# GpSimd in place of VectorE for scaling the softmax probabilities and for the differential subtraction, in a two-block transformer kernel on one core

## The reference, cut to what matters

```python
# differential heads (4 heads, two maps each, per layer)
p = jax.nn.softmax(s, axis=-1)
a = p[:, 0] - lam * p[:, 1]
return jnp.einsum('bhqs,bshd->bqhd', a.astype(v.dtype), v)
...
# latent (mla), cross (x) and grouped (gqa) heads; windowed (swa) heads add exp(sink - m) to the sum
p = jax.nn.softmax(s, axis=-1)
return jnp.einsum('bhqs,bshd->bhqd', p.astype(v.dtype), v)
```

## Time and profile before

| what | value |
|---|---|
| median of 3 runs | 1756.21 us (1754.52 to 1757.25) |
| span of the profiled execution | 1752.8 us |
| what lies around that span | not given for this execution; the median less its span is 3.4 us |
| PE busy | 1572.7 us (90%) |
| DVE busy | 802.2 us (46%) |
| ACT busy | 374.8 us (21%) |
| POOL busy | 2.2 us |
| HBM read | 383.65 MB |

### The profile page before, as it was taken

The page is one execution under the profiler, slowest core; times in us unless marked ns, Lnnn a source line. Parts: engine busy times, 40 slices in busy tenths (PEclk is TensorE's granted clock), DMA queues, the critical chain, the costliest instruction groups (busy, mean ns, idle before and its releaser), DMA issues.

```text
span 1752.8 us, 25923 instructions
## 1 busy us (share of the span) xinstructions
PE 1572.7 (90%) x10722; PEld 1084.5 (62%) x10722; DVE 802.2 (46%) x1623; ACT 374.8 (21%) x943; POOL 2.2 (0%) x6
## 2 busy tenths in 40 slices
PE   9999999999999999999999999999999656656666
PEld 5877878884488786888648778888853112112111
DVE  6686567665577765766646575242421000000001
ACT  4362131110325422311002561111211000000001
POOL 0000000000000000000000000000000000000000
PEclk9999999999999999999999999999999977788767
DMA  9324335444542241544444223221888999999997
GB/s 394 127 73 168 121 121 209 160 177 173 201 169 94 96 169 72 203 174 162 177 172 162 103 100 119 74 73 53 335 337 329 427 423 424 425 425 426 423 421 326
DMA packets 49472, 386.35 MB, mean 220 GB/s; under 512 B 5584, under 2 KB 6096, under 8 KB 9808
## 3 DMA queue, kind: packets, MB, share of 16 engines
q1 hardware_dynamic: 47376, 375.15, 54.0%
q10 hardware_dynamic: 1984, 9.57, 1.4%
HBM read 383.65 MB, written 1.05 MB: 219 GB/s over the span
## 4 chain that ended last, share of the span: by engine, by line
PE 72%; DMA 21%; DVE 3%; ACT 2%; issue 1%; DVEq 0%; SPq 0%; ACTq 0%
PE ps L212 52%; DMA arena<-in_stream 21%; PE ps L2347 3%; PE ps L1090 2%; PE ps L1579 2%; PE ps L216 1%; PE ps L1189 1%; PE ps L739 1%; PE ps L1222 1%; PE ps L1248 1%; PE ps L1680 0%; PE ps L640 0%; PE ps L2429 0%; PE ps L1030 0%; PE ps L2486 0%
## 5 line engine op out<-in xcount | busy, mean ns | idle before, releaser
L212 PE MATMUL ps<-arena 128*128 128x256 f32 (+4 forms) x2364 | 532.7, 491 | 88.0 <-DMA arena<-in_stream 78.3
L212 PEld LDWEIGHTS ps<-arena 128*128 128x128 f32 (+1 forms) x2364 | 308.5, 172 | 270.9 <-DMA arena<-in_stream 131.5
L212 PE MATMUL ps<-ring,arena 128*128 128x256 f32 (+5 forms) x1172 | 319.1, 497 | 35.3 <-DMA ring<-in_stream 29.4
L212 PE MATMUL ps<-arena,ring 128*128 128x256 f32 (+1 forms) x1212 | 274.4, 374 | 0.0
L212 PEld LDWEIGHTS ps<-ring,arena 128*128 128x128 f32 (+1 forms) x1172 | 177.7, 173 | 150.9 <-issue 75.4
L212 PEld LDWEIGHTS ps<-arena,ring 128*128 128x128 f32 x1212 | 216.2, 191 | 35.5 <-issue 9.6
L2906 DVE TENSOR_TENSOR arena<-arena,ps 128x512 f32<-128x512 f32 x8 | 5.5, 687 | 308.9 <-PE ps L2684 308.9
L2684 PE MATMUL ps<-arena 128*32 128x512 f32 x218 | 139.8, 769 | 0.0
L1137 ACT ACTIVATE arena<-arena,small 128x256 f32<-128x256 f32 x112 | 55.7, 498 | 67.0 <-DVE small L1124 50.5
L1726 ACT ACTIVATE arena<-arena 128x512 f32<-128x512 f32 x20 | 12.6, 630 | 179.4 <-DVE arena L1782 179.4
L1090 PE MATMUL ps<-arena 64*128 64x256 f32 (+3 forms) x256 | 46.8, 392 | 0.8 <-DVE arena L1120 0.5
(11 more groups left out here) (461 smaller groups left out, 1994.5 us busy)
## 6 DMA issues: line engine op xcount, KB each, us to landing
ring<-in_stream SPq DMA_DIRECT2D x131, 1024.0 KB, 4.9
arena<-in_stream SPq DMA_DIRECT2D x112, 1024.0 KB, 13.0
arena<-in_stream SPq DMA_DIRECT2D x24, 2048.0 KB, 37.2
ring<-in_stream SPq DMA_DIRECT2D x12, 2048.0 KB, 32.4
spare<-in_stream SPq DMA_DIRECT2D x6, 2048.0 KB, 37.0
par<-in_stream SPq DMA_DIRECT2D x8, 1024.0 KB, 38.7
const<-in_stream SPq DMA_DIRECT2D x8, 1024.0 KB, 38.7
par<-in_layer_par ACTq DMA_DIRECT2D x3, 1664.0 KB, 8.0
```

The lines of the kernel that those rows point to most:

```text
L212: ins = self.pe.e.matmul(out, lhsT, rhs, start=start, stop=stop)
```

## The change

Every scaling of probabilities and every differential subtraction moves from DVE's program to POOL's. DVE keeps the inversion of the sums (and the sink term and the factor lambda) and then raises a new semaphore, `sums_inverted`, which is shared by all stages and counted on through them. POOL waits for it, scales both row blocks, and for diff m = 1 waits for its own scaling, subtracts, and raises `probs_scaled`, on which PE and ACT wait as before. POOL's program now starts with the items of both layers (`layer_pool`), then its two memsets, then the gqa items. The operands, shapes and buffers of the moved instructions are the same.

```diff
+LAYER_ITEMS = len(HEAD_ITEMS + X_ITEMS)
+SUMS_BEFORE = {"layer_0": 0, "layer_1": LAYER_ITEMS, "second": DEPTH * LAYER_ITEMS}
...
-def softmax_scale_dve(p, dve, i, item):
+def softmax_invert_dve(p, dve, i, item):
...
-    dve.e.reciprocal(sums[:, 0:2], sums[:, 0:2]).then_inc(dve.step(), 1)
-    dve.e.wait_ge(dve.steps, dve.n)
     if kind == "diff" and m == 1:
-        dve.e.tensor_scalar(sums[:, 0:2], sums[:, 0:2], p.lam[:, 0:1], None, ALU.mult).then_inc(dve.step(), 1)
+        dve.e.reciprocal(sums[:, 0:2], sums[:, 0:2]).then_inc(dve.step(), 1)
         dve.e.wait_ge(dve.steps, dve.n)
+        dve.e.tensor_scalar(sums[:, 0:2], sums[:, 0:2], p.lam[:, 0:1], None, ALU.mult).then_inc(dve.event("sums_inverted"), 1)
+    else:
+        dve.e.reciprocal(sums[:, 0:2], sums[:, 0:2]).then_inc(dve.event("sums_inverted"), 1)
+
+
+def softmax_scale_pool(p, pool, i, item):
+
+    kind, h, m = item
+    pool.e.wait_ge(p.sem("sums_inverted"), sums_before(p) + i + 1)
+    sums = p.sums[:, 4 * (i % 8):4 * (i % 8) + 4]
+    pr = p.pr[i % 4]
     for b in range(NB):
-        ins = dve.e.tensor_scalar(pr[:, b, :], pr[:, b, :], sums[:, b:b + 1], None, ALU.mult)
+        ins = pool.e.tensor_scalar(pr[:, b, :], pr[:, b, :], sums[:, b:b + 1], None, ALU.mult)
         if kind == "diff" and m == 1 or b < NB - 1:
-            ins.then_inc(dve.step(), 1)
+            ins.then_inc(pool.step(), 1)
         else:
-            ins.then_inc(dve.event("probs_scaled"), 1)
+            ins.then_inc(pool.event("probs_scaled"), 1)
     if kind == "diff" and m == 1:
 
-        dve.e.wait_ge(p.sem("probs_scaled"), i)
-        dve.e.wait_ge(dve.steps, dve.n)
-        dve.e.tensor_tensor(p.pr[(i - 1) % 4], p.pr[(i - 1) % 4], pr, ALU.subtract).then_inc(dve.event("probs_scaled"), 1)
+        pool.e.wait_ge(p.sem("probs_scaled"), i)
+        pool.e.wait_ge(pool.steps, pool.n)
+        pool.e.tensor_tensor(p.pr[(i - 1) % 4], p.pr[(i - 1) % 4], pr, ALU.subtract).then_inc(pool.event("probs_scaled"), 1)
+
+
+def layer_pool(p, pool):
+
+    for i, item in enumerate(HEAD_ITEMS + X_ITEMS):
+        softmax_scale_pool(p, pool, i, item)
...
-            softmax_scale_dve(p, dve, n0 + t - 1, items[t - 1])
+            softmax_invert_dve(p, dve, n0 + t - 1, items[t - 1])
```

More of the change, by code:

```diff
@@ L1142, in softmax_exp_act, with sums_before @@
             ins.then_inc(act.step(), 1)
-def softmax_scale_dve(p, dve, i, item):
+def sums_before(p):
+    return SUMS_BEFORE[p.stage]
+def softmax_invert_dve(p, dve, i, item):
     kind, h, m = item
@@ L1149, in softmax_scale_dve @@
     sums = p.sums[:, 4 * (i % 8):4 * (i % 8) + 4]
-    pr = p.pr[i % 4]
     if kind == "swa":
@@ L2440, in low_rank @@
     def low_rank(name, src, e):
-        pe.e.wait_ge(p.sem("lora_in"), 1)
+        pe.e.wait_ge(p.sem("head_inputs"), 1)
         for j in range(2):
@@ L2464, in beside_head @@
         if t == 3:
-            head_sums(p.kd, "squares", 1)
+            head_sums(p.kd, "head_inputs", 2)
             low_rank("a2", 13, 1)
@@ L2493, in second_pe @@
         if m == 0:
-            head_sums(p.kd, "bonus_in", 1)
+            head_sums(p.kd, "recurrence_in", 2)
         for n in range(6):
@@ L2959, in second_act @@
     act.e.activation(p.shifted[:, 12, :], p.shifted[:, 12, :], ACT.Tanh).then_inc(act.step(), 1)
-    act.e.activation(p.shifted[:, 14, :], p.shifted[:, 14, :], ACT.Sigmoid).then_inc(act.event("lora_in"), 1)
+    act.e.activation(p.shifted[:, 14, :], p.shifted[:, 14, :], ACT.Sigmoid).then_inc(act.event("head_inputs"), 1)
     p.gate_seen = 0
@@ L3009, in after_head @@
                 if q == PAIRS - 1:
-                    ins.then_inc(act.event("squares"), 1)
+                    ins.then_inc(act.event("head_inputs"), 1)
                 else:
@@ L3256, in key_sum @@
             if q == 3:
-                ins.then_inc(dve.event("bonus_in"), 1)
+                ins.then_inc(dve.event("recurrence_in"), 1)
             else:
@@ L3512, in second_pool @@
     pool.e.memset(flat(p.zp[1]), 0.0).then_inc(pool.event("pads_zeroed"), 1)
+    for i, item in enumerate(GQA_ITEMS):
+        softmax_scale_pool(p, pool, i, item)
 def build(nc, stream, x, mem, pos_row, pos_col, const, layer_par, out):
@@ L3521, in build @@
         loads = ["const_loaded", "const_rest", "mem_loaded", "x_loaded_0", "x_loaded_1", "positions_loaded", "layer_params", "layer_rest"]
-        p.share(*loads, "y_final", "stored", "down_first", "recurrence_left", "branches_left")
+        p.share(*loads, "y_final", "stored", "down_first", "recurrence_left", "branches_left", "sums_inverted")
         block = ctx.enter_context(nc.Block())
@@ L3578, in _ @@
             pool = Engine(p, e, "pool")
+            for l in range(DEPTH):
+                p.stage = f"layer_{l}"
+                layer_pool(p, pool)
             p.stage = "second"
```

## The result

The changed kernel takes **1768.59 us** in the median of 4 runs (1768.45 to 1770.9) against 1756.73 us of the kernel before beside it. The ratio is 1.0078 with a 95% interval of 1.0067 to 1.009: slower, as forecast, but past the top of the range, 1766.6 us. Run again as experiment e10_changed it has 1768.8 us against 1755.3 us, 13.5 us more. The profiled execution shown here took 1770.9 us, its span is 1769.0 us. Two executions in all were slow ones, one of the kernel before beside experiments 1 to 4 (8893 us) and one of e4_spread (1934 us); the ratios leave them out, and the medians without them would be 1755.38 for 1755.49 us and 1758.65 for 1758.71 us.

The account below looks back on a forecast made before the run. PE was taken to bound the heads, 99.7% busy. A vanished wait of -0.4 us and +4.4 us of waits at the diff items gave +4.0 us on 1756.2, so 1760.2 us; range 1754.5 to 1766.6.

Parts of the forecast that it names:

- The price of a scaling: POOL's time for one 256-column scaling, estimated from its memsets as a read pass plus a write pass: 0.5 us.
- the outer end: Upper cost of a POOL scaling, three passes, 0.74 us; PE then waits 8.4 us in all at the diff items.
- The frame: Diff items 5, 7, 9, 11: POOL's 2.5 us chain against 1.8 to 2.2 us available; PE waits, +4.4 us in two layers.
- The subtraction: POOL's 128x512 differential subtraction in diff items, m = 1, estimated at 1.3 us.
- the wait gained: PE's wait for DVE before the scores of items 12 and 13 goes: 0.2 us in each layer, -0.4 us.
- the cover of the swa, cross and gqa items: These items need 1.1 us for two scalings and hand-overs and have 2.2 us or more, so PE does not wait.
- DVE's relief at nothing: Some 40 us of work leaves DVE, almost none on the path; relief in the gqa heads costed at nothing.
- The hand-overs: Three in a diff item (to POOL, from scalings to subtraction, to PE), 0.06 us each, 0.18 us together.
- Item 0: Layer's first item: 1.1 us needed, 1.4 us available, so no wait; 0.2 us in each layer at 0.74 us for a scaling.
- The exclusion rival: DVE's weight sums keep POOL out of SBUF at item 19; PE waits 2.0 us in two layers, 1762.2 us; chance 0.20.
- The prediction's last sign: If small DVE instructions (negated maxima) grow or start late beside POOL, exponentials come late too; costed at nothing.
- The quick rival: One-pass POOL scaling of 0.31 us, diff chain 2.2 us: 1757.8 us, no change that can be told; chance 0.27.

Follow-up runs that it names:

- e10_changed: The changed kernel run again as it is, beside more runs of the kernel before: 1768.8 us against 1755.3 us, ratio 1.0075.
- experiments 1 to 4: Changed kernel with diff items on DVE, only diff items on POOL, item 19 on DVE, or DVE's weight sums delayed: 1758.42, 1765.01, 1766.34, 1769.05 us.
- e4_spread: Changed kernel with one two-input 128x512 multiply, sums spread over the columns, in place of the two scalings everywhere: 1758.71 us, ratio 1.0016 to the kernel before.
- e9_prices: Changed kernel with gqa items 3 to 5 in other forms (one 128x512 scaling, four of 128x128, a copy), for prices alone: 1768.8 us, single run.
- e8_with_room: Changed kernel with only 68 scalings on POOL; diff items and items 0, 1 and 19 stay on DVE: 1755.96 us, ratio 1.0000 to the kernel before.
- e6_sums_after: Changed kernel, but DVE's weight sums wait until POOL has scaled item 19: 1769.05 us, ratio 1.0074 to the kernel before.
- e7_sub_pool: Kernel before with only the 8 subtractions moved to POOL, all scalings on DVE: 1755.1 us, ratio 0.9995.

## Why the prediction was right and wrong

**The price of a scaling failed.** The step was "If the passes do not overlap, a scaling takes 0.10 + 2 x 0.214 = 0.52 us", from which 0.5 us was taken, with three passes, 0.74 us, as the outer end. It is 0.92 us: 0.29 fixed and, for each column, three times the memset's 0.835 ns (e9_prices). To count one pass for the read and one for the write fits neither form: a copy, which does both, has the slope of one pass, and the scaling that of three. The memset's fixed part was no ruler either. The outer end had three passes but kept 0.10 us fixed, so it missed by the 0.19 us of that and the range's top with it. A POOL slower than the outer end had been given a chance of 0.05. In a chain with two scalings 0.92 in place of 0.5 is 2 x 0.42 = 0.84 us.

**The frame held.** By the frame I mean where the time is lost: a chain on POOL against the time that PE leaves it. Put the measured chain of 3.38 us into the prediction's own times: items 5, 7, 9 and 11 wait 1.2, 1.5, 1.5 and 1.6 us, 5.8 us in a layer. Two things come off. The weight load takes 0.42 us after a wait and 0.57 where it runs beside earlier products, which gives back 0.15 four times: from the load of item 7 to the next scores it is 0.59 us (100.58 to 101.17) against 0.74 before (97.54 to 98.28). And item 9's 0.2 us was a gain. That leaves 5.0; measured are 4.9. The subtraction (1.3 forecast, 1.26 measured), the wait gained (0.2 in a layer), the cover of the swa, cross and gqa items (no wait) and DVE's relief at nothing (e8_with_room) all stand. The hand-overs sum to 0.29 us, not 0.18: the one between two of POOL's own instructions, 0.14, had no row. One reading was off without consequence: the three runs of before lie 1.7 us below and 1.0 above their median, not 1.3 around it, which moves only the lower end of the range.

**Item 0** was given 1.4 us of room and "0.2 us in each layer" at the outer end. At 1.82 us for its pair and the hand-overs of 0.15 us it is short by 0.57, and costs 0.5. The sentence that a scaling over 0.74 us "brings waits to the swa items as well" was wrong but for item 19: 2 x 0.92 + 0.15 = 2.0 us fits into the 2.2 of item 13.

**The exclusion rival was true** and came on top of the forecast, as it said. It was priced at 1.0 us in a layer, with a ready time of 129.15 + 1.1; with scalings of 0.92 it costs 1.3. It had been given 0.20 although no row of before spoke against it. The Trainium skill (SBUF — State Buffer, SBUF: two separate sides) has the rule that a VectorE instruction with two inputs in SBUF and a GpSimd instruction that reads SBUF exclude each other. The trace agrees, with 3.81 us for 1.83 at item 19, 1.82 once DVE holds still (e6_sums_after), and DVE held up by 0.84 us where POOL gets in between (e4_spread). The prediction's last sign, small DVE instructions such as the negated maxima that grow beside POOL, was seen too (for 0.17 us, 0.26 at most in the changed kernel, 0.58 in e7_sub_pool and 1.17 in e4_spread), and no wait of PE ends with it.

**The quick rival was refuted.** The Trainium skill (GPSIMD Engine Reference, 4.1 Engine selection) puts one-input work roughly at line rate and two-input work at about twice VectorE's time. For two inputs the traces agree: the subtraction takes 1.26 us to VectorE's 0.69, 1.8 times. For the one-input scaling they don't: it takes 0.92 us to VectorE's 0.35, 2.6 times, and two inputs of 256 columns take 0.61 us, less than one input and a sum. Of the one-input forms only the copy, 0.40 us, is quick.

**The sum.** Forecast: -0.4 + 4.4 = +4.0 us. Measured in the profiles: 2 x (0.5 + 4.9 + 1.3) = 13.4 us. Of the 9.4 us between them, 5.8 are the diff chain (two layers of 4.9, less 4.0), nearly all by the scaling's price, 1.0 is item 0 by the same price, and 2.6 are item 19 by the exclusion.

## What to carry to other kernels

Where PE is full, as here, relief of another engine gains next to nothing (one wait of 0.2 us in a layer), and what decides is each tile's own time from ready input to due output: 68 scalings moved free of charge, 44 others and the 8 subtractions cost 13 us. Price an operation on GpSimd by its own form, not by another instruction of the engine; when no row shows it, widen the fixed part as well as the slope, since a chain holds it several times. Before moving work there, look at what VectorE runs beside it: here instructions with two operands in SBUF on VectorE stopped GpSimd (item 19), and GpSimd stopped one of those (e4_spread) and small one-operand ones too (e7_sub_pool).

## What the runs showed of the hardware

- On GpSimd a `tensor_scalar` with one sum for each partition costs 0.29 us and 2.5 ns for each column (0.60, 0.92 and 1.56 us for 128, 256 and 512 columns); by a number it is 0.85 us for 256. A `tensor_tensor` that spreads the same sums does all 512 columns in 1.04 us, where two `tensor_scalar` need 1.83.
- Small VectorE instructions suffer from the exclusion too. The addition of two sums, 128x2, of the swa items took 153 ns in the median and 161 at most before. Beside POOL:

```profile
L1158 DVE TENSOR_TENSOR small<-small x16: 152/166/399, 111.4 to 595.5; 128x2 f32<-128x2 f32 x16
```

- With one operand in SBUF the exclusion shows as well. The 128x2 negation of the maxima (L1118 before, 169 ns in the median and 171 at most) ended in e7_sub_pool and e4_spread 0.02 to 0.03 us after the subtraction of POOL that ran beside it, after up to 1.17 us:

```profile
102.83 1.26 POOL L1215 TENSOR_TENSOR arena<-arena 128x512 f32<-128x512 f32 x1
102.95 1.17 DVE L1120 TENSOR_SCALAR small<-small 128x2 f32<-128x2 f32 x1
```

  Beside POOL's scalings it took 0.26 us at most, and the reciprocals of the same size were not held up (151 to 180 ns). What tells the one from the other wasn't tested.
- VectorE instructions that read one operand from PSUM (the maxima) took 0.42 us beside POOL's scalings, 0.43 at most, as they did before.
- The last gqa item's two scalings, which run beside several two-operand products of VectorE, took 5.59 us in e9_prices, three times their price, and no wait of PE there ends with them.
